# One-core encoder layer: the weight loads of the experts in another order in the queue

## The chip, the cores and the metric

The kernel runs on one core of one Trainium2 chip. The metric is the device time of one execution in microseconds (us); less is better. The core's engines are TensorE (PE in the profile, its weight loads PEld), VectorE (DVE), ScalarE (ACT), GpSimd (POOL) and SyncE (SP). SyncE computes nothing here: it waits on semaphores and issues DMAs, which 16 DMA engines carry out. "SPq" in a row is SyncE's sequencer.

## The reference

One encoder layer over 512 tokens of width 1024: three attention branches, a gated merge, and then the part that matters here, a layer of 32 experts of which each token uses four.

```python
def expert_block(args):
    xb, e = args
    gu = xb @ w_gu[e] + b_gu[e]                      # 1024 x 2048 per expert
    g = jnp.minimum(gu[:, :D_EXPERT], SWIGLU_LIMIT)
    lin = jnp.clip(gu[:, D_EXPERT:], -SWIGLU_LIMIT, SWIGLU_LIMIT)
    act = g * jax.nn.sigmoid(SWIGLU_ALPHA * g) * (lin + 1.0)
    return act @ w_down[e] + b_down[e]               # 1024 x 1024 per expert
```

Everything is float32. An expert's first matrix has 8 MB and its second 4 MB.

## The kernel before

The tokens of an expert are cut into jobs of up to 96 slots; there are 32 jobs here, numbered 0 to 31, and each job reads its expert's two matrices from HBM once. The first matrix comes in four pieces of 2 MB, the second in two. SBUF holds two full sets of four pieces for the first matrix (`gu_pair`, set 0 and set 1, taken in turn by even and odd jobs) and one set of two pieces for the second (`dn_pair`).

TensorE's order is fixed: `gate_up(0)`, and then in each step j `gate_up(j + 1)` (192 matmuls, L1783) followed by `down(j)` (192 matmuls, L1799), two steps to an iteration of its loop; after the loop come `gate_up(31)`, `down(30)` and `down(31)`. A part is one slice of weights: `gate_up` has eight parts and `down` four, and each part ends with an increment of `gemm_ps`. Two parts read one 2 MB piece, so a piece is free again when its second part is done. `gate_up` waits for each piece's `gu_in`, `down` for each piece's `dn_in`.

All weight loads are issued by SyncE, in one program order, onto one queue. SyncE waits until `gemm_ps` shows that a piece is free (`wait_part`) and then issues the next load into it. In the steady loop before the change, while step j runs, SyncE waits in `down(j)` for its two pieces, issues the two loads for `down(j + 1)` into them as they come free (after the second and the fourth part), and only then issues the four loads for `gate_up(j + 3)`, into pieces that `gate_up(j + 1)` had freed earlier in the same step:

```python
for m in range(GU_PAIRS):
    wait_part(sp, i, b * PARTS + 2 * m + 1)
    if m == 0:
        load_bias(e_gu, b)
    load_gu(e_gu, b, m)
for m in range(DN_PAIRS):
    wait_part(sp, i, stream(b, KD + 2 * m + 1))
    load_dn(e_dn, m)
```

GpSimd shares the same 16 DMA engines: in each step it adds the job's outputs to rows in HBM (`x_rows`, L964, small packets) and gathers the tokens of a coming job (`xq`, L958). These loads have a queue of their own ("software_dynamic", q0; SyncE's is q1, "hardware_dynamic").

Of the kernel before, what the change touches and what calls it, by code (L numbers as in the profile page):

```python
# [20 lines left out]
KD = D // P  # L21
# [11 lines left out]
N_EXP = 32  # L33
# [78 lines left out]
def encoder_kernel(nc, x, mem, norm_mix, w_in, q_norm_a, k_norm_a, sink_b, norm_mem, w_mem_kv,  # L112
# [3 lines left out]
    with ctx:  # L116
# [60 lines left out]
        def small(name, shape, dt):  # L177
            nonlocal at
            t = sb(name, shape, dt, at)
            size = int(np.prod(shape[1:])) * (2 if dt == BF16 else 4)  # L180
            at += -(-size // 32) * 32
            return t
# [105 lines left out]
        job_table = small("job_table", [1, 2, 64], I32)  # L288
# [258 lines left out]
        DN_PARTS = KD // 2  # L547
        GU_PAIRS = KD // 2
        DN_PAIRS = DN_PARTS // 2
        PARTS = KD + DN_PARTS  # L550
        G1 = GEMMS[UNITS]

        def stream(b, p):

            return KD + b * PARTS + p

        def wait_part(eng, i, m):
            eng.wait_ge(gemm_ps, i * (2 * PARTS) + (G1 + m + 1))
# [4 lines left out]
        def _(sp):  # L563
# [46 lines left out]
            def load_gu(e, s, m):  # L610
                sp.dma_start(gu_pair[s * GU_PAIRS + m][:], wgu[e, m, :, :]).then_inc(gu_in[s * GU_PAIRS + m], 16)

            def load_dn(e, m):
                sp.dma_start(dn_pair[m][:], wdn[e, m, :, :]).then_inc(dn_in[m], 16)

            def load_bias(e, s):
                for g in range(TRIOS):
                    sp.dma_start(bias_row[s][QUARTER * g:QUARTER * g + 8, :], bias_parts[e].rearrange("q r h n -> (q r) (h n)")).then_inc(bias_row_in[s], 16)
# [23 lines left out]
            e_one = sp.value_load(job_table[0:1, 0, 1:2], min_val=0, max_val=N_EXP - 1)  # L642
# [4 lines left out]
            sp.wait_ge(gate_t_ps, 1)  # L647
            load_gu(e_one, 1, GU_PAIRS - 1)
            pairs_but_one = sp.value_load(job_table[0:1, 1, 1:2], min_val=MIN_PAIRS - 1, max_val=NJ // 2 - 1)
            with sp.Fori(0, pairs_but_one) as i:  # L650
                for b in range(2):
                    e_gu = sp.value_load(job_table[0:1, 0, bass.ds(i * 2 + b + 2, 1)], min_val=0, max_val=N_EXP - 1)
                    e_dn = sp.value_load(job_table[0:1, 0, bass.ds(i * 2 + b + 1, 1)], min_val=0, max_val=N_EXP - 1)
                    for m in range(GU_PAIRS):
                        wait_part(sp, i, b * PARTS + 2 * m + 1)
                        if m == 0:
                            load_bias(e_gu, b)
                        load_gu(e_gu, b, m)
                    for m in range(DN_PAIRS):
                        wait_part(sp, i, stream(b, KD + 2 * m + 1))  # L660
                        load_dn(e_dn, m)
            e_last = sp.value_load(job_table[0:1, 0, bass.ds(pairs_but_one * 2 + 1, 1)], min_val=0, max_val=N_EXP - 1)
            wait_part(sp, pairs_but_one, stream(0, KD - 1))
            sp.dma_start(final_gain[:], norm_final.rearrange("(a n) -> a n", a=1).to_broadcast([P, D])).then_inc(fgain_in, 16)
# [18 lines left out]
        def _(act):  # L683
# [60 lines left out]
            def take_item(n):  # L744
                kind, _, slot = ITEMS[n]
                bank = 4 + n % 2 if n < 4 else 6 + (ITEM_STEP[n] // TB + 1) % 2
                act.wait_ge(qk_ps, n + 1)
                nc.scalar.activation(k_t[:] if kind == "k" else q_t[:, slot, :], ps[:, bank, :], ACT.Copy).then_inc(qk_done, 1)
# [1142 lines left out]
```

## Time and profile before

| | |
|---|---|
| median of 3 runs | 1474.77 us (1473.94 to 1475.23) |
| the profiled execution's own time | 1475.15 us |
| its span, first to last instruction | 1473.2 us |
| outside the span | 1.95 us |
| TensorE busy | 1448.4 us, 98% |
| VectorE, GpSimd, ScalarE busy | 464.4, 295.0, 270.4 us |
| moved by the DMA engines | 468.90 MB, of it 450.40 MB on SyncE's queue |

The expert stage runs from about 436 us to the end. Busy time of TensorE is modelled from the starts of its matmuls, so a high share alone doesn't say that it never waits; the idle time ahead of a group, and the chain that ended last, say more. "DMA share" in a row is the mean busy share of the 16 DMA engines; it can read a little over 1 where the packets of two queues overlap on an engine. One engine alone is a share of 0.0625.

### The profile page before, as it was taken

What the parts mean: (1) busy time and instruction counts of PE and PEld (TensorE: products, weight loads), DVE (VectorE), ACT (ScalarE), POOL (GpSimd) and SP (SyncE); (2) the same over time, 40 slices, a digit from 0 to 9 for tenths busy, and PEclk for the clock granted to TensorE, in tenths of its full rate; (3) what the DMA queues carried; (4) which work ended last, traced back from release to release, by engine and by line L of the source; (5) the groups of instructions that cost most, each with busy time, mean ns of one, the idle gap of its engine ahead of it and who ended that gap; (6) DMA issues with size and microseconds to landing.
All of it is one profiled execution on the core that took longest, in us unless ns stands there. A gap on an engine that the chain in (4) does not pass through costs nothing.

```text
span 1473.2 us, 34231 instructions
## 1 busy us (share of the span) xinstructions
PE 1448.4 (98%) x14951; PEld 754.4 (51%) x14951; DVE 464.4 (32%) x683; ACT 270.4 (18%) x491; POOL 295.0 (20%) x384
## 2 busy tenths in 40 slices
PE   8999999999999999999999999999999999999997
PEld 7876588888874344333344333344333344333344
DVE  4848833324561122211122211122211122211124
ACT  5458842233111010000010000010000010000011
POOL 0000040000012222233222233222233222232211
PEclk9999999999989999999999999999999999999999
DMA  7320013224959699999999999999999999999976
GB/s 257 138 86 1 23 49 123 90 72 138 377 211 419 255 413 418 413 415 412 415 420 414 417 416 412 416 415 416 418 413 412 415 417 414 419 414 412 414 292 243
DMA packets 71692, 468.90 MB, mean 318 GB/s; under 512 B 16040, under 2 KB 24772, under 8 KB 47040
## 3 DMA queue, kind: packets, MB, share of 16 engines
q1 hardware_dynamic: 52064, 450.40, 74.3%
q0 software_dynamic: 19104, 17.73, 5.5%
q8 instruction: 32, 0.52, 0.1%
q10 hardware_dynamic: 480, 0.15, 0.0%
q14 instruction: 12, 0.10, 0.0%
HBM read 458.33 MB, written 19.79 MB: 325 GB/s over the span
## 4 chain that ended last, share of the span: by engine, by line
PE 95%; DVE 3%; DMA 1%; ACT 0%; issue 0%; ACTq 0%; DVEq 0%; SPq 0%
PE ps L1783 45%; PE ps L1799 22%; PE ps L1433 7%; PE ps L1435 7%; PE ps L1434 7%; PE ps L1460 2%; PE ps L1586 1%; DVE head_max L1102 1%; PE ps L1774 1%; PE ps L1542 1%; DVE probs L1120 1%; DMA dn_pair<-in_w_down 1%; PE ps L1704 1%; PE ps L1469 0%; PE ps L1689 0%; DMA gain_rows<-in_norm_ffn 0%
## 5 line engine op out<-in xcount | busy, mean ns | idle before, releaser
L1783 PE MATMUL ps<-gu_pair,xt 128*32 128x512 f32 x6144 | 666.0, 593 | 0.5 <-ACT xt L859 0.5
L1783 PEld LDWEIGHTS ps<-gu_pair,xt 128*32 128x32 f32 x6144 | 197.1, 110 | 447.5 <-issue 446.7
L1799 PE MATMUL ps<-dn_pair,act_t 128*32 128x256 f32 x6144 | 339.1, 381 | 0.5 <-DMA dn_pair<-in_w_down 0.5
L1799 PEld LDWEIGHTS ps<-dn_pair,act_t 128*32 128x32 f32 x6144 | 201.0, 111 | 146.0 <-issue 20.2
L1336 DVE TENSOR_SCALAR lin_sb<-ps 128x768 f32<-128x768 f32 x32 | 30.6, 958 | 638.4 <-ACT sg_sb L865 638.4
L964 POOL DMA_INDIRECT x_rows<-y_sb,sum_row x93 | 147.9, 1591 | 37.8 <-issue 37.8
L941 POOL TENSOR_TENSOR mark_sb<-ones 1x1 f32<-1x1 f32 x93 | 30.3, 326 | 622.9 <-DVE y_sb L1352 617.8
L865 ACT ACTIVATE sg_sb<-ps,limits 128x768 f32<-128x768 f32 x32 | 28.8, 900 | 631.2 <-PE ps L1783 631.2
L1433 PE MATMUL ps<-w_high,h_hi 128*128 128x512 f32 x352 | 138.4, 393 | 0.6 <-DVE mem_lo L1048 0.5
L1435 PE MATMUL ps<-w_high,h_lo 128*128 128x512 f32 x352 | 137.3, 390 | 0.0
L1434 PE MATMUL ps<-w_low,h_hi 128*128 128x512 f32 x352 | 137.2, 390 | 0.0
L958 POOL DMA_INDIRECT xq<-h_rows,gather_row x93 | 96.6, 1039 | 38.2 <-issue 37.4
L518 DVE TENSOR_TENSOR w_low<-w_raw,w_high 128x2048 fp32r<-128x2048 f32 (+2 forms) x36 | 63.9, 1813 | 117.7 <-ACT w_high L510 117.7
L1433 PEld LDWEIGHTS ps<-w_high,h_hi 128*128 128x128 f32 x352 | 66.1, 188 | 14.8 <-DVE mem_lo L1048 0.8
L1435 PEld LDWEIGHTS ps<-w_high,h_lo 128*128 128x128 f32 x352 | 66.1, 188 | 13.9
L1434 PEld LDWEIGHTS ps<-w_low,h_hi 128*128 128x128 f32 x352 | 66.2, 188 | 13.2
L1352 DVE TENSOR_TENSOR y_sb<-ps,y_gate 128x768 f32<-128x768 f32 x31 | 29.7, 957 | 133.9 <-PE ps L1799 133.9
L870 ACT ACTIVATE y_gate<-slot_gates 128x3 f32 x32 | 6.6, 205 | 284.9 <-DVE y_sb L1352 280.4
L510 ACT ACTIVATE w_high<-w_raw 128x2048 fp32r<-128x2048 f32 (+2 forms) x36 | 53.5, 1538 | 20.3 <-PE ps L1435 17.6
L1344 DVE SCALAR_TENSOR_TENSOR act_sb<-lin_sb,sg_sb 128x768 f32<-128x768 f32 x32 | 48.9, 1528 | 3.3
L1332 DVE STREAM_TRANSPOSE xt<-xq 128x768 f32<-128x768 f32 x30 | 47.7, 1589 | 0.0
L972 POOL MEMSET limits<- 128x1 f32 x1 | 0.1, 98 | 215.8 <-DVE h L1181 215.8
(252 smaller groups left out, 962.5 us busy)
## 6 DMA issues: line engine op xcount, KB each, us to landing
gu_pair<-in_w_gate_up SPq DMA_DIRECT2D x128, 2048.0 KB, 22.2
dn_pair<-in_w_down SPq DMA_DIRECT2D x64, 2048.0 KB
w_raw<-in_w_in SPq DMA_DIRECT2D x8, 2048.0 KB, 8.0
w_raw<-in_w_out SPq DMA_DIRECT2D x2, 2048.0 KB, 7.7
w_raw<-in_w_in SPq DMA_DIRECT2D x2, 1024.0 KB, 8.1
x_sb<-in_x SPq DMA_DIRECT2D x8, 256.0 KB, 7.4
w_raw<-in_w_mem_kv SPq DMA_DIRECT2D x1, 2048.0 KB, 11.1
x<-in_x SPq DMA_DIRECT2D x4, 512.0 KB, 5.2
```

Source lines behind the costliest of these rows:

```text
L510: nc.scalar.activation(wh[u % 2][:, a * COLS:b * COLS], raw[u % 2][:, a * COLS:b * COLS], ACT.Copy).then_inc(wh_done, 1)
L518: nc.vector.tensor_tensor(wl[u % 2][:, a * COLS:b * COLS], raw[u % 2][:, a * COLS:b * COLS], wh[u % 2][:, a * COLS:b * COLS].bitcast(F32), ...
L958: nc.gpsimd.indirect_dma_start(out=xq[s][:, g, :], out_offset=None, in_=h2_rows.rearrange("r (q n) -> (r q) n", q=4), in_offset=bass.Indir ...
L964: nc.gpsimd.indirect_dma_start(out=x_rows.rearrange("r (q n) -> (r q) n", q=4), out_offset=bass.IndirectOffsetOnAxis(ap=sum_row[:, s, g:g ...
L1332: nc.vector.transpose(xt[:].rearrange("p g k t -> p (g k) t"), xq[s][:].rearrange("p g (i k) -> p g k i", k=KD)).then_inc(xt_done, 1)
L1336: nc.vector.tensor_scalar(lin_sb[:], ps[:, 0:TRIOS, QCOLS:2 * QCOLS], LIMIT, -LIMIT, ALU.min, ALU.max).then_inc(l_ready, 1)
L1344: nc.vector.scalar_tensor_tensor(out=act_sb[:].rearrange("p (c x) -> p x c", c=KD), in0=lin_sb[:].rearrange("p g (i c) -> p (g i) c", c=KD ...
L1433: nc.tensor.matmul(bank, hi, w_hi, start=start, stop=False)
L1434: nc.tensor.matmul(bank, hi, w_lo, start=False, stop=False)
L1435: return nc.tensor.matmul(bank, lo, w_hi, start=False, stop=stop)
L1783: last = nc.tensor.matmul(ps[quarter(q), g, :], xt[:, g, k, :], w.rearrange("p (h n) -> p h n", h=2)[:, :, q * QCOLS:(q + 1) * QCOLS], sta ...
L1799: last = nc.tensor.matmul(ps[quarter(q), bank + g, 0:QCOLS], act_part(2 * c + h, g), dn_w[c][:, h * D + q * QCOLS:h * D + (q + 1) * QCOLS] ...
```

## The change

Only SyncE's program changes. The four loads for `gate_up(j + 3)` are now issued one by one while `gate_up(j + 1)` reads the pieces, that is ahead of `down(j)` and ahead of the two loads for `down(j + 1)`. No load is added or removed, and no other engine's program changes.

```diff
-            with sp.Fori(0, pairs_but_one) as i:
+
+            def job_weights(i, b, e_gu, e_dn):
+                for m in range(GU_PAIRS):
+                    wait_part(sp, i, b * PARTS - DN_PARTS + 2 * m + 1)
+                    if m == 0:
+                        load_bias(e_gu, b)
+                    load_gu(e_gu, b, m)
+                for m in range(DN_PAIRS):
+                    wait_part(sp, i, b * PARTS + DN_PARTS + 2 * m + 1)
+                    load_dn(e_dn, m)
+
+            e_two = sp.value_load(job_table[0:1, 0, 2:3], min_val=0, max_val=N_EXP - 1)
+            for m in range(GU_PAIRS):
+                wait_part(sp, 0, 2 * m + 1)
+                if m == 0:
+                    load_bias(e_two, 0)
+                load_gu(e_two, 0, m)
+            e_three = sp.value_load(job_table[0:1, 0, 3:4], min_val=0, max_val=N_EXP - 1)
+            job_weights(0, 1, e_three, e_one)
+            with sp.Fori(1, pairs_but_one) as i:
                 for b in range(2):
                     e_gu = sp.value_load(job_table[0:1, 0, bass.ds(i * 2 + b + 2, 1)], min_val=0, max_val=N_EXP - 1)
-                    e_dn = sp.value_load(job_table[0:1, 0, bass.ds(i * 2 + b + 1, 1)], min_val=0, max_val=N_EXP - 1)
-                    for m in range(GU_PAIRS):
-                        wait_part(sp, i, b * PARTS + 2 * m + 1)
-                        if m == 0:
-                            load_bias(e_gu, b)
-                        load_gu(e_gu, b, m)
-                    for m in range(DN_PAIRS):
-                        wait_part(sp, i, stream(b, KD + 2 * m + 1))
-                        load_dn(e_dn, m)
+                    e_dn = sp.value_load(job_table[0:1, 0, bass.ds(i * 2 + b, 1)], min_val=0, max_val=N_EXP - 1)
+                    job_weights(i, b, e_gu, e_dn)
+            e_next = sp.value_load(job_table[0:1, 0, bass.ds(pairs_but_one * 2, 1)], min_val=0, max_val=N_EXP - 1)
+            for m in range(DN_PAIRS):
+                wait_part(sp, pairs_but_one, DN_PARTS + 2 * m + 1)
+                load_dn(e_next, m)
```

Inside the loop both programs issue four loads of a first matrix and then two of a second. What differs is which second matrix follows which first one, and that is decided where the loop is entered. On SyncE, the first time that a second matrix is loaded in the stage, the program before has these rows (`dn_pair` 166 and 167 are the two pieces of the second matrix, `gu_pair` 158 to 161 set 0 and 162 to 165 set 1 of the first):

```order
L614 DMA dn_pair_167<-in_w_down 128x4096
L652 ISA
L652 TENSOR_LOAD job_table
L652 ISA x2
L653 TENSOR_LOAD job_table
L653 ISA x2
L558 REGISTER_ALU
L618 ISA [waits gemm_ps]
L618 DMA bias_row_113<-bias_parts 8x512 x3
L611 ISA
L611 DMA gu_pair_162<-in_w_gate_up 128x4096
```

The second matrix of job 1 stands ahead of the first matrix of job 3, which goes into set 1. At the same place the changed program has:

```order
L618 DMA bias_row_113<-bias_parts 8x512 x3
L611 ISA
L611 DMA gu_pair_162<-in_w_gate_up 128x4096
L611 ISA [waits gemm_ps]
L611 DMA gu_pair_163<-in_w_gate_up 128x4096
L611 ISA [waits gemm_ps]
L611 DMA gu_pair_164<-in_w_gate_up 128x4096
L611 ISA [waits gemm_ps]
L611 DMA gu_pair_165<-in_w_gate_up 128x4096
L614 ISA [waits gemm_ps]
L614 DMA dn_pair_166<-in_w_down 128x4096
```

Job 3's first matrix has moved ahead of job 1's second, and each of its loads has a wait of its own. The loop keeps this order to its end. Behind the loop, on SyncE, the program before goes straight to the loads of the tail:

```order
L662 ISA
L662 TENSOR_LOAD job_table
L662 ISA x2
L558 ISA
L664 DMA final_gain<-in_norm_final 128x1024 [waits gemm_ps]
L666 DMA down_bias<-in_b_down 32x1024 x4
L558 REGISTER_ALU
L614 ISA [waits gemm_ps]
L614 DMA dn_pair_166<-in_w_down 128x4096
```

and the changed program first issues the second matrix of job 30, which no first matrix precedes any more:

```order
L674 ISA
L674 TENSOR_LOAD job_table
L674 ISA x2
L558 ISA
L614 ISA [waits gemm_ps]
L614 DMA dn_pair_166<-in_w_down 128x4096
L558 REGISTER_ALU
L614 ISA [waits gemm_ps]
L614 DMA dn_pair_167<-in_w_down 128x4096
```

So each second matrix but the last two has one first matrix more ahead of it in the queue than before.

## Rows read from the trace of the kernel before

**Rows 1.** The page: busy time, and the two groups of expert matmuls (last field: idle time before)

```profile
PE 1448.4 (98%) x14951; PEld 754.4 (51%) x14951; DVE 464.4 (32%) x683; ACT 270.4 (18%) x491; POOL 295.0 (20%) x384
...
L1783 PE MATMUL ps<-gu_pair,xt 128*32 128x512 f32 x6144 | 666.0, 593 | 0.5 <-ACT xt L859 0.5
...
L1799 PE MATMUL ps<-dn_pair,act_t 128*32 128x256 f32 x6144 | 339.1, 381 | 0.5 <-DMA dn_pair<-in_w_down 0.5
```

**Rows 2.** The chain that ended last, late jobs: start, length, what

```profile
1368.92 10.36 PE ps L1799 x192
...
1379.71 20.74 PE ps L1783 x192
1400.45 10.36 PE ps L1799 x192
...
1437.37 8.03 DMA dn_pair<-in_w_down
...
1445.44 12.30 PE ps L1799 x192
```

**Rows 3.** SyncE's timeline, first jobs: start, length, what is issued

```profile
453.17 9.09 SPq L611 DMA_DIRECT2D gu_pair<-in_w_gate_up  x4
491.41 5.51 SPq L614 DMA_DIRECT2D dn_pair<-in_w_down  x2
...
499.84 1.99 SPq L611 DMA_DIRECT2D gu_pair<-in_w_gate_up  x4
522.94 5.51 SPq L614 DMA_DIRECT2D dn_pair<-in_w_down  x2
```

**Rows 4.** SyncE's timeline, last jobs

```profile
1374.30 5.51 SPq L614 DMA_DIRECT2D dn_pair<-in_w_down  x2
...
1382.72 2.00 SPq L611 DMA_DIRECT2D gu_pair<-in_w_gate_up  x4
1405.83 5.51 SPq L614 DMA_DIRECT2D dn_pair<-in_w_down  x2
...
1437.37 5.54 SPq L614 DMA_DIRECT2D dn_pair<-in_w_down  x2
```

**Rows 5.** The third load of three first matrices: when issued, and time to landing

```profile
L611 SPq DMA_DIRECT2D gu_pair<-in_w_gate_up x1: 333/333/333, 501.0 to 501.0; - x1
...
DMA to landing us min/median/max: 21.4/21.4/21.4
...
L611 SPq DMA_DIRECT2D gu_pair<-in_w_gate_up x1: 333/333/333, 1194.7 to 1194.7; - x1
...
DMA to landing us min/median/max: 30.3/30.3/30.3
...
L611 SPq DMA_DIRECT2D gu_pair<-in_w_gate_up x1: 333/333/333, 1383.9 to 1383.9; - x1
...
DMA to landing us min/median/max: 32.7/32.7/32.7
```

**Rows 6.** Stretches in early jobs: engines' busy time, clock, DMA share, GB/s

```profile
478.00:479.00 1.00, 1.00 (x15) 0.28 (x10) 0.00 (x0) 0.00 (x0) 0.00 (x0) 1.00 0.84 305
...
481.50:492.00 10.50, 10.50 (x160) 5.07 (x156) 4.78 (x4) 1.84 (x2) 0.00 (x0) 1.00 0.01 2
```

**Rows 7.** The same view, end of the job loads

```profile
1431.00:1432.00 1.00, 1.00 (x16) 0.34 (x12) 0.00 (x0) 0.00 (x0) 0.00 (x0) 1.00 0.08 34
1432.00:1433.00 1.00, 1.00 (x24) 0.64 (x20) 0.00 (x0) 0.87 (x1) 0.00 (x0) 1.00 0.01 1
```

**Rows 8.** DMA over one job, 1347.67 to 1379.20 us, and a GpSimd add later

```profile
DMA packets 1468, 13.04 MB, mean 414 GB/s; under 512 B 298, under 2 KB 598, under 8 KB 718
...
q0 software_dynamic: 576, 0.70, 9.4%
...
1412.92 1.63 POOL L964 DMA_INDIRECT x_rows<-y_sb,sum_row  x1 [0.55 <-issue]
```

**Rows 9.** The stretch behind TensorE's wait near the end

```profile
1446.00:1458.00 12.00, 11.69 (x188) 6.42 (x180) 0.00 (x0) 0.24 (x1) 3.77 (x3) 0.86 0.82 265
```

## The prediction

> **What bounds the kernel now.** I read the page first. TensorE is busy for 1448.4 of 1473.2 us, and the idle time ahead of both groups of expert matmuls is 0.5 us in all [rows 1]. Busy time is modelled, so this alone proves little. The chain of work that ended last settles it: `down` starts at 1368.92 and again at 1400.45 us, 31.53 us apart, and the chain stays on TensorE between them [rows 2]. So a job costs 31.53 us of matmuls in the loop, and no wait for a weight is in it. Only at the end does the chain go over a load: 8.03 us for the second matrix of job 31, of which about 5.2 us lie beside the second half of `down(30)`.
>
> Second question: how close are the loads to being late? Over one job the DMA engines move 13.04 MB at 414 GB/s [rows 8], which is 31.5 us. The loads are thus almost as long as the matmuls. The landing times tell more. A load has landed when the slowest of its 16 shares has. The third load of a first matrix landed 21.4 us after its issue at 501.0 us, 30.3 us after it at 1194.7, and 32.7 us after it at 1383.9 [rows 5]. Issue stands in the same place of a job each time, so the backlog grows by (32.7 - 21.4) / 28 jobs = 0.40 us per job: the slowest share needs 31.53 + 0.40 = 31.93 us of work for each job. The end of the stage shows how few engines this concerns: between 1431 and 1432 us the DMA share is 0.08, little more than one engine of 16, and that one is done at about 1432.2 (share 0.01 in the next us) [rows 7]. I call it the last engine. Before the change its backlog is harmless: it is never late by the time at which TensorE reads.
>
> The Trainium skill, "DMA: Bandwidth & Descriptors", section "Latency and other measured facts", says that DMA engines 7 and 15 are usually slower than the others. The rows don't name the engine, but that one or two lag agrees with it.
>
> **The change, part by part.** TensorE, ScalarE, VectorE and GpSimd keep their programs: 0 us. SyncE issues as many loads as before; it has some 20 us of waiting between its groups of issues [rows 4], which hides its extra waits and table reads: 0 us. Memory is the same.
>
> What it adds to a second matrix is queue. Each share of a load waits behind the earlier loads on its engine. Before, the second matrix of job 30 (issued at 1405.83) was the last behind the first matrix of job 31 (1382.72), and the one of job 29 (1374.30) stood ahead of it [rows 4]. Now job 31's first matrix stands ahead of job 29's second.
>
> *What has to be done by when.* The second piece of job 29 is read from the third part of `down(29)` on: 1400.45 + 10.36 / 2 = 1405.6 us [rows 2]. After the change, everything up to the first matrix of job 31 and the second of job 29 has to be through by then. Before, the last engine was through this same set of loads when the fourth load of job 31's first matrix had landed. The third landed at 1383.9 + 32.7 = 1416.6 [rows 5]; three loads later, at 1432.2, it was done with everything [rows 7], so 15.6 / 3 = 5.2 us per load, and the fourth landed at 1421.8.
>
> *What it gains at the start.* The queue was empty once. Job 2's first matrix was issued from 453.17 us, and then nothing until 491.41 [rows 3]. The share falls from 0.84 in 478 to 479 us and is 0.01 over 481.5 to 492 [rows 6]: the first engines ran dry at about 478.3, the last at about 481.3, and with 1.1 us from issue to the first packets (taken as the start at 492.5, where that stretch ends) they stood still for 11 to 14 us. The changed program issues job 3's first matrix from about 470 us, while `gate_up(1)` reads, so this gap fills, and from then on the last engine is ahead of its former self by 11 to 14 us. The engine that lags at the end most likely lagged at the start too, so I take 11.5.
>
> *What else shifts.* The q0 traffic takes 9.4% of the engines' time, 3.0 us per job [rows 8]. It is tied to TensorE's time, not to the queue. The adds issued from 1412.92 us on [rows 8] slowed the load that landed at 1421.8; in the new order it is past before they come. I take a quarter of a job's 3.0 us, 0.7 (0 to 1.5).
>
> *The sum.* 1421.8 - 11.5 - 0.7 = 1409.6 us, against a need at 1405.6: **4.0 us late**. By the same working at the load issued at 1194.7: 1194.7 + 30.3 + 5.2 - 12.2 = 1218.0, need 189.1 us before 1405.6, i.e. 1216.5: 1.5 us late. So the first wait should come some four jobs earlier, near 1090 us, and from then on each job waits 0.4 us for its second matrix. The ends: advance 14 and shift 1.5 give 0.7 us, advance 11 and shift 0 give 5.2.
>
> *Given back?* Job 30's second matrix has no first matrix ahead of it any more, and job 31's is issued and lands as before, 8.03 us later [rows 2, 4]. Nothing behind job 29 is late, and nothing makes up the 4.0 us: the matmuls of the rest lie on the chain. First matrices come earlier, but no `gate_up` waited for one (0.5 us idle in all, and that on ScalarE [rows 1]), so earlier arrival gains 0.
>
> Against the profiled execution (1473.2 us span, 1475.15 with what lies around it) this makes 1477.2 and 1479.15. That execution is 0.4 us over the median, so I forecast 1474.8 + 4.0 = **1478.8 us**.
>
> *The rule that speaks against the change.* The last engine's landing times grow steadily though TensorE takes weights at a constant pace [rows 5]: a load waits for all that was issued ahead of it. The Trainium skill, "DMA: Bandwidth & Descriptors", section "Queues, rings and completion order", says that on each DMA engine descriptors are consumed in ring order. Without the gap at the start this rule would make the sum 11.5 us larger, 15.5 us late; the empty stretch in this case's trace [rows 6] cuts it to 4.0.
>
> **The rivals.**
>
> *No wait at all: same time.* For it: only about one engine is late by this much (share 0.08 near the end [rows 7]), and if its extra work comes from four loads issued within 2 us [rows 4] beside the adds, evenly spread loads may take less than 31.93 us per job. It decides if it needs 31.93 - 4.0 / 28 = 31.79 us or less per job: a third less drift, 0.26 instead of 0.40. Also, runs without the profiler may drift less than this one. Against it: the growth is steady, (30.3 - 21.4) / 22 = 0.40 us per job up to 1194.7 and (32.7 - 30.3) / 6 = 0.40 from there on [rows 5]. Time: 1474.8 us.
>
> The Trainium skill, "DMA: Bandwidth & Descriptors", section "Where 436 GB/s comes from", gives a ceiling of 435.2 GB/s. An estimate from it is 13.04 MB / 435.2 GB/s = 30.0 us per job, under the matmuls' 31.53; by that rule the queue would never grow and the change would cost 0. The measured 414 GB/s and the growing landing times [rows 5, 8] say otherwise for the slowest share, and the measurement decides.
>
> *Larger loss.* If TensorE's waits bring its clock down: behind the wait near the end, the granted clock is 0.86 over 12 us [rows 9], a loss of 12 x 0.14 = 1.7 us, with part of it at 1.2 instead of 2.4 GHz. That wait comes out of 8.03 us in which TensorE had only 5.2 us of work. Waits of 0.4 us are far smaller and I don't expect it; if three or four did it, 4.0 + 3.5 x 1.7 gives about +10 us, 1484.8.
>
> *Faster.* The change would have to take away a wait that is in the chain. There is one for weights, the 8.03 us ahead of `down(31)`, and its issue hangs on `down(30)` in both programs. If the last engine's earlier finish cut a bit of the landing time, at most 8.03 - 5.2 = 2.8 us could go; that needs a queue that still holds it up at 1437, and it was empty since 1432.2 but for the small loads of the tail. Time then 1472.0.
>
> *The change does nothing.* Excluded: the order of issue shows the first matrix ahead of the second.
>
> **How the numbers follow.** A measurement of this kernel tells about 0.2% from no change, 2.95 us. The waits as worked out (0.7 to 5.5 us): 0.66, of which 0.13 is under 2.95 us. No wait: 0.24. Larger loss: 0.07. Faster: 0.03. So slower 0.53 + 0.07 = 0.60, same 0.13 + 0.24 = 0.37, faster 0.03. The range goes from the no-wait case, 1474.3 with the spread of the runs, to 1480.8, a little over the upper end of the sum; the larger loss stays out. The forecast's own range is 1475.5 to 1480.3.
>
> **What the changed profile would show.** The engines busy at 481.5 to 492 us (share near 1). Job 1's second matrix landing some 16 us after its issue (481.3 + 5 loads x 5.3 = 507.8, issued at 491.4), and job 29's 26 us after it, when it is needed (1400.45 - 1374.30). In the chain, from about 1090 us on, pieces "DMA dn_pair" between `gate_up` and `down`, or a `down` longer than 10.36 us, 0.4 us per job and 4 us in all; `gate_up` unchanged; clock at 1.00 in the loop. The last load for job 29 is the last late one. I am wrong if `down` stays at 10.36 us everywhere (the last engine's drift is smaller in the new order), if waits are there from the first jobs (no gap was filled), or if it is `gate_up` that waits.

## The result, and the profile after

The changed kernel takes 1480.59 us (median of 6 runs, 1479.15 to 1482.51) against 1475.21 (1473.94 to 1475.68, 6 runs): ratio 1.0038, 95% interval 1.0026 to 1.0050. It is slower by 5.4 us. The profiled execution took 1482.51 us, with a span of 1480.7.

The page of the changed kernel has TensorE still at 98%. What has moved is the idle time ahead of the matmuls of `down` (last field, L1815 here, L1799 before), where [rows 1] had 0.5 us, and that of their weight loads:

```profile
L1799 PE MATMUL ps<-gu_pair,xt 128*32 128x512 f32 x6144 | 667.4, 594 | 0.5 <-ACT xt L875 0.5
...
L1815 PE MATMUL ps<-dn_pair,act_t 128*32 128x256 f32 x6144 | 341.0, 381 | 3.7 <-DMA dn_pair<-in_w_down 3.5
L1815 PEld LDWEIGHTS ps<-dn_pair,act_t 128*32 128x32 f32 x6144 | 199.1, 110 | 153.6 <-DMA dn_pair<-in_w_down 15.0
```

`gate_up` waits for nothing, as before. Ahead of a wait, the sequencer still has matmuls in the array, so the 3.5 us of matmul idle time and the 15.0 us of weight-load idle time (20 waits) frame the loss. The chain gives it more closely. It stays on TensorE until 1117 us, job after job as in [rows 2], and then:

```profile
1117.31 5.18 PE ps L1815 x96
...
1122.51 5.43 PE ps L1815 x96
...
1128.10 26.58 DMA dn_pair<-in_w_down
...
1154.72 5.43 PE ps L1815 x96
...
1160.30 26.36 DMA dn_pair<-in_w_down
...
1379.37 26.75 DMA dn_pair<-in_w_down
...
1406.16 10.57 PE ps L1815 x192
...
1417.17 20.74 PE ps L1799 x192
...
1443.29 8.41 DMA dn_pair<-in_w_down
```

The chain hardly runs through `gate_up` any more: from 1128 to 1379 us it goes from the issue of a second piece to its landing 26.4 to 26.8 us later, then through half a `down`, which frees the piece for the next issue (only at 1353 us does it pass through one `gate_up`, and behind it, for `down(29)`, it is the first piece that is late). Two such steps start 1160.30 - 1128.10 = 32.2 us apart, the later ones 32.0 to 32.1, where matmuls alone need 31.53. `down(29)` starts at 1406.16, against 1400.45 in [rows 2]; 0.66 us of that was there before the loop (465.96 against 465.30 us for the start of `gate_up(1)`): in this execution TensorE idled 2.34 us for the gather of the first tokens, its granted clock was at the lower level (0.51) from 434.9 to 438.4 us, and the first 72 matmuls of `gate_up(0)` took 9.36 us instead of 7.93. `down(29)` ends at 1416.73, where before it ended at 1410.81: with the 0.66 off, 5.3 us are lost in the loop. The other 1.6 us by which the two spans differ lie behind it (0.4 of it in the last second matrix, 8.41 instead of 8.03 us, and 1.2 behind `down(31)`). The medians, 5.4 us apart, are close to the loop's loss alone.

The view of stretches shows that stretch of lower clock (first line) and the gap of [rows 6] filled:

```profile
434.90:438.40 3.50, 3.01 (x16) 0.79 (x20) 3.12 (x5) 0.44 (x1) 2.25 (x2) 0.51 0.49 112
...
478.00:479.00 1.00, 1.00 (x16) 0.32 (x12) 0.00 (x0) 0.00 (x0) 0.30 (x1) 1.00 1.03 363
...
481.50:492.00 10.50, 10.50 (x156) 4.77 (x148) 4.12 (x4) 1.84 (x2) 0.00 (x0) 1.00 1.01 422
```

and the third load of a first matrix, the view of [rows 5], is issued some 15 to 20 us earlier and needs as long as all that stands in the queue. The three are the loads of jobs 3, 25 and 31:

```profile
L611 SPq DMA_DIRECT2D gu_pair<-in_w_gate_up x1: 333/333/333, 481.7 to 481.7; - x1
DMA to landing us min/median/max: 15.5/15.5/15.5
...
L611 SPq DMA_DIRECT2D gu_pair<-in_w_gate_up x1: 333/333/333, 1176.3 to 1176.3; - x1
DMA to landing us min/median/max: 25.8/25.8/25.8
...
L611 SPq DMA_DIRECT2D gu_pair<-in_w_gate_up x1: 333/333/333, 1368.9 to 1368.9; - x1
DMA to landing us min/median/max: 26.3/26.3/26.3
```

### The profile page after: what moved, and what is told of

The parts are those of the page before. It is cut to its first block, busy times and chain, and to the rows that moved or that the text cites. A ratio compares the mean times of both kernels' runs of the same rounds, so it can differ in the third digit from the quotient of the medians.

```text
span 1480.7 us, 34258 instructions
## 1 busy us (share of the span) xinstructions
PE 1447.7 (98%) x14951; PEld 746.5 (50%) x14951; DVE 464.1 (31%) x683; ACT 270.5 (18%) x491; POOL 295.0 (20%) x384
## 3 DMA queue, kind: packets, MB, share of 16 engines
q0 software_dynamic: 19104, 17.73, 5.5%
## 4 chain that ended last, share of the span: by engine, by line
PE 80%; DMA 16%; DVE 3%; issue 0%; ACT 0%; ACTq 0%; DVEq 0%; SPq 0%; POOLq 0%
PE ps L1799 34%; PE ps L1815 20%; DMA dn_pair<-in_w_down 15%; PE ps L1449 7%; PE ps L1451 7%; PE ps L1450 7%; PE ps L1476 2%; PE ps L1602 1%; DVE head_max L1118 1%; PE ps L1558 1%; PE ps L1790 1%; DVE probs L1136 1%; DMA xg<-h_rows,gather_row 0%; PE ps L1485 0%; PE ps L1705 0%
## 5 line engine op out<-in xcount | busy, mean ns | idle before, releaser
L1799 PE MATMUL ps<-gu_pair,xt 128*32 128x512 f32 x6144 | 667.4, 594 | 0.5 <-ACT xt L875 0.5
L1799 PEld LDWEIGHTS ps<-gu_pair,xt 128*32 128x32 f32 x6144 | 196.7, 110 | 449.4 <-issue 448.5
L1815 PE MATMUL ps<-dn_pair,act_t 128*32 128x256 f32 x6144 | 341.0, 381 | 3.7 <-DMA dn_pair<-in_w_down 3.5
L1815 PEld LDWEIGHTS ps<-dn_pair,act_t 128*32 128x32 f32 x6144 | 199.1, 110 | 153.6 <-DMA dn_pair<-in_w_down 15.0
```

Source lines behind the costliest of these rows:

```text
L1799: last = nc.tensor.matmul(ps[quarter(q), g, :], xt[:, g, k, :], w.rearrange("p (h n) -> p h n", h=2)[:, :, q * QCOLS:(q + 1) * QCOLS], sta ...
L1815: last = nc.tensor.matmul(ps[quarter(q), bank + g, 0:QCOLS], act_part(2 * c + h, g), dn_w[c][:, h * D + q * QCOLS:h * D + (q + 1) * QCOLS] ...
```

## The experiments

Eight kernels tell the order in the queue, the gap at the start, the spacing and the traffic apart; three more (e3, e9, e10) vary the dose. Times are medians beside runs of the kernel before on the same chip.

### e1: second matrices on a queue of their own

```diff
-                for m in range(DN_PAIRS):
-                    wait_part(sp, i, b * PARTS + DN_PARTS + 2 * m + 1)
-                    load_dn(e_dn, m)
...
                     sigmoid(j + 1)
+                    e_dn = act.value_load(job_table[0:1, 0, bass.ds(i * 2 + b + 1, 1)], min_val=0, max_val=N_EXP - 1)
+                    for m in range(DN_PAIRS):
+                        wait_part(act, i, stream(b, KD + 2 * m + 1))
+                        act.dma_start(dn_pair[m][:], wdn[e_dn, m, :, :]).then_inc(dn_in[m], 16)
```

> The changed kernel, with the second matrices of jobs 1 to 30 issued by ScalarE on its own queue instead of by SyncE; same bytes, same 16 engines, first matrices as early as in the changed kernel. My theory (a second matrix is late because one first matrix more stands ahead of it in the same queue): on a queue of its own it shares each engine with the first matrices instead of waiting behind them, so about 2 us + 2 x 4.9 us = 12 us from issue to landing against the 26 us at which it is needed; no wait ahead of down, 31.53 us per job to the end, 1475.2 us. Rival (the last DMA engine can't carry the loads of a job in a job's time, whatever their order): down still waits from about 1120 us on, 1480 us. If ScalarE's issuing costs time of its own, it shows in down or in the sigmoid, not as a wait for dn_pair.

Measured: 1474.57 us against 1474.62, ratio 0.9995 (0.9986 to 1.0005). Its chain at the place where the changed kernel loses time, and ScalarE's issue in the timeline:

```profile
1368.96 10.36 PE ps L1812 x192
1379.32 0.43 PE ps L1787 x3
1379.76 20.74 PE ps L1796 x192
1400.49 10.36 PE ps L1812 x192
...
712.18 5.51 ACTq L902 DMA_DIRECT2D dn_pair<-in_w_down  x2
```

The first matrices are issued as early as in the changed kernel and the same 16 engines carry the same bytes, but a job takes 31.53 us again. The loss thus came from what stands ahead in the one queue. By the landing records, a first piece took 14.1 to 14.8 us from issue to its slowest share and a second one 18.3 to 19.8 (jobs 1 to 29), more than the 12 that I expected and well under 26. The last engine still falls behind in e1: the third load of a first matrix lands 17.3 us after its issue for job 3 and 37.1 us after it for job 31. The lateness has moved to loads that can bear it; it hasn't gone.

### e2: the gap at the start kept

```diff
             e_three = sp.value_load(job_table[0:1, 0, 3:4], min_val=0, max_val=N_EXP - 1)
+            wait_part(sp, 0, DN_PARTS + PARTS + 1)
             job_weights(0, 1, e_three, e_one)
```

> The changed kernel, with the first matrix of job 3 held back until down(0) has read its first piece (about 491 us), so that the DMA engines stand still as long as in the kernel before; the order in the queue is that of the changed kernel. My theory (backlog: the early issue gave the last engine 11.5 us of advance against 21 us more ahead of each second matrix): without the advance TensorE is 11.5 us later than in the changed kernel, 1480.6 + 11.5 = 1492 us, with waits ahead of down from the first jobs on (second matrix of job 1 landing some 27 us after issue). Rival (only the growth per job counts, not where it starts): 1480.6 us, first wait near 1120 us.

Measured: 1498.76 us against 1474.62, ratio 1.0160 (1.0143 to 1.0177), 18 us over the changed kernel. The stretch is empty again, and the chain waits at the first chance:

```profile
481.50:492.00 10.50, 10.50 (x168) 5.15 (x164) 4.87 (x4) 1.84 (x2) 0.00 (x0) 1.00 0.01 3
...
495.20 26.70 DMA dn_pair<-in_w_down
...
521.95 13.07 PE ps L1816 x192
```

`down(1)` takes 13.07 us instead of 10.36, and that is the clock: TensorE idled 4.95 us before it, from 517.0 to 521.95 us, its granted clock was at the lower level (0.50) from 520.2 to 527.0 us, and `down(1)` got through only 48 of its 192 matmuls in the 5.05 us of that stretch in which it ran.

```profile
521.95 13.07 PE L1816 MATMUL ps<-dn_pair,act_t 128*32 128x256 f32 x192 [4.95 <-DMA dn_pair<-in_w_down]
...
520.20:527.00 6.80, 5.05 (x48) 2.37 (x52) 2.76 (x2) 0.00 (x0) 0.00 (x0) 0.50 1.01 398
```

The second piece had landed by 527.5 us, before `down(1)` came to it. Where the backlog starts decides, as my theory had it; the rival is out. The size was off: not 11.5 but 18 us. By the landing records 14.6 of them stand at job 1's second matrix (through at 527.5 us, against 513.0 in the changed kernel), and the rest has come by job 29's (1428.9 against 1411.0).

### e3, e9, e10: some pieces ahead, the others behind

```diff
-                for m in range(GU_PAIRS):
+                for m in range(GU_PAIRS // 2):
                     wait_part(sp, i, b * PARTS - DN_PARTS + 2 * m + 1)
...
                     load_dn(e_dn, m)
+                for m in range(GU_PAIRS // 2, GU_PAIRS):
+                    load_gu(e_gu, b, m)
```

with 1 and 3 in the place of `GU_PAIRS // 2` in e9 and e10.

> The changed kernel, with the third and fourth piece of each first matrix issued behind the second matrix, the first two ahead of it. My theory: 2 x 5.2 = 10.4 us less stand ahead of a second matrix, and the gap at the start fills nearly as well, so the end of job 29's load comes some 9 us earlier than in the changed kernel, 4 us ahead of its need; no wait at all, 1475.2 us. Rival (each piece moved ahead costs its share): half the loss, 1478 us.

Measured: 1478.95 us against 1474.62, ratio 1.0030 (1.0021 to 1.0040). Both expectations failed: half the dose costs 4.3 us, four fifths of the whole loss. The backlog began as low as I had worked out (the first one landed 8.6 us after issue at 492 us), but it grew nearly twice as fast, and the waits came all the same:

```profile
1211.38 10.59 PE ps L1817 x192
...
1222.12 26.91 DMA dn_pair<-in_w_down
```

> The changed kernel with one piece of each first matrix issued ahead of the second matrix and three behind it. The last engine's backlog grew by 0.46 us per job with no piece ahead, 0.8 with two (e3) and 0.55 with four. Theory A (the growth comes with cutting the first matrix in two parts around the second): 0.7 to 0.8 us here, from 9 us at first to 26 us some 22 jobs later, then waits, 1478 to 1479 us. Theory B (it grows with what stands ahead): 0.5 us, 23 us at the end, no wait, 1475 us.

Measured: 1482.06 us against 1475.39, ratio 1.0044 (1.0027 to 1.0061), growth 1.0 us per job: more than either theory.

> The same with three pieces ahead and one behind. 15.6 us more ahead, of which 11.5 filled the gap at the start: the second matrix of job 1 lands some 13 us after issue. Theory A (cut in two): 0.7 to 0.8 us of growth per job, the need of 26 us reached after 17 jobs and 11 jobs of waits, 1482 to 1484 us, more than the changed kernel's. Theory B: growth 0.5 us, reached after 26 jobs, 1476 us.

Measured: 1476.69 us against 1475.39, ratio 1.0007 (0.9998 to 1.0017), growth 0.65 us. Theory A had the time much too long; theory B had the time (1476 us) and the place at which waits begin (1311 us, 26 jobs on), but not the growth. The loss is not a matter of how many pieces are moved: 0, 1, 2, 3, 4 pieces ahead cost 0, 6.7, 4.3, 1.3 and 5.4 us, of which the times alone don't tell 1.3 from nothing; that e10 waits is seen in its trace, where `down` is idle 1.9 us for `dn_pair`.

### e4, e11: the spacing of the issues

e4 is the kernel before with its first matrices issued 5.2 us apart, e11 the changed kernel with them issued two and two:

```diff
-                        wait_part(sp, i, b * PARTS + 2 * m + 1)
+                        wait_part(sp, i, b * PARTS + KD + 2 * m + 1)
...
-                    wait_part(sp, i, b * PARTS - DN_PARTS + 2 * m + 1)
+                    wait_part(sp, i, b * PARTS - DN_PARTS + 4 * (m // 2) + 3)
```

> The kernel before, in its order, but each piece of a first matrix is issued a part of gate_up later, 5.2 us apart, instead of four at once behind down. It asks why the last engine's backlog grew by 0.55 us per job after the change and 0.40 before. If the spacing of the issues is the cause: 0.55 us per job here too. If it is the order or what stands in the queue: 0.40 us per job. Either way second matrices land 9 us after issue at first and at most 24 at the end, under the 26 they have, so no wait and 1475.2 us.

Measured: 1474.87 us against 1474.62, ratio 1.0003 (0.9993 to 1.0013). The first pieces of its second matrices landed 11.0 us after issue at 489 us and 22.6 at 1403, which is 0.40 us per job.

> The changed kernel in its order, but the four loads of a first matrix are issued two and two (after the fourth and the eighth part of gate_up) instead of one by one. If only the order in the queue and the bytes count: as the changed kernel, growth 0.55 us per job, 1480 to 1481 us. If the evenly spaced issue is what raised the growth from 0.46 to 0.55: growth 0.46 to 0.50, some 2 us less, 1478 to 1479 us.

Measured: 1481.11 us against 1475.39, ratio 1.0041 (1.0027 to 1.0055). With the order before, spacing the issues brings neither waits nor faster growth; with the new order, bunching them takes neither away (waits begin at 999 us, even earlier than at 1122). Even spacing is out as a cause, of the loss and of the faster growth.

### e5 to e8: GpSimd's traffic left out

One bound is changed, in `add_rows` for e5 and e7 and in `gather_quarters` for e6 and e8; e5 and e6 start from the changed kernel, e7 and e8 from e3:

```diff
-                                                 in_=y_sb[:, g, :], in_offset=None, bounds_check=4 * SEQ - 1, oob_is_err=False,
+                                                 in_=y_sb[:, g, :], in_offset=None, bounds_check=0, oob_is_err=False,
```

> The changed kernel, with the bounds of GpSimd's adds into x_rows set so that they write next to nothing (the experts' outputs of jobs 0 to 30 are left out of the result; every wait and every matmul stays). In the changed kernel the last engine needs about 32.1 us of work per job against 31.53 us of matmuls. My theory: that overload is the traffic of GpSimd's queue on top of 6 x 4.9 us = 29.4 us of weights; the adds take 30 us of packet time per job, 1.9 us per engine. Without them about 30.2 us per job, so the backlog shrinks from job to job instead of growing, no wait ahead of down, 1475 us. Rival (the weight loads alone are too slow on that engine): waits from about 1120 us on as before, 1480 us.

> The changed kernel, with the bounds of GpSimd's gathers of the tokens of jobs 2 to 31 set so that they read next to nothing (those jobs compute with old data; waits and matmuls stay). The gathers take 15 us of packet time per job, 1.0 us per engine. My theory: 32.1 - 1.0 = 31.1 us per job on the last engine, under 31.53, no waits, 1475 us. It also asks what makes some of the 16 KB weight packets slow (mean 620 ns against 611 at best, most of the excess in the stretch in which the gathers run): if it is the gathers, the excess in that stretch goes and the engine has still more room; if it stays, something else makes it.

Measured: 1474.91 us (ratio 1.0005, 0.9995 to 1.0014) without the adds and 1475.07 (1.0004, 0.9994 to 1.0013) without the gathers, against 1474.64. Their pages, e5 first, show what was taken off the queue (17.73 MB and 5.5% of the engines' time in the changed kernel) and that `down` has next to no wait left:

```profile
q0 software_dynamic: 19104, 9.80, 2.4%
...
L1815 PE MATMUL ps<-dn_pair,act_t 128*32 128x256 f32 x6144 | 339.1, 380 | 0.8 <-DMA dn_pair<-in_w_down 0.8
```

```profile
q0 software_dynamic: 19104, 9.85, 4.3%
...
L1815 PE MATMUL ps<-dn_pair,act_t 128*32 128x256 f32 x6144 | 339.1, 380 | 1.0 <-DMA dn_pair<-in_w_down 1.0
```

By the landing records, a second matrix took 14 to 16 us in the first jobs and 9.0 and 9.5 at 1348 us: the backlog shrinks. In the changed order the weights with one kind of GpSimd's traffic are not too much for the last engine, with both kinds they are; the rival, that the weights alone are too much, is out.

> The kernel with two pieces ahead (e3), adds left out as in e5. In e3 the last engine's backlog grew by 0.8 us per job instead of 0.46, with a mean weight packet of 624 ns instead of 619. Theory A: slower weight packets come from meeting the gathers; they stay at some 624 ns here, and the backlog no longer grows because 1.9 us of adds per job are gone. Theory B: they come from meeting the adds; the mean falls to some 615 ns. Either way no wait, 1475 us.

> The kernel with two pieces ahead (e3), gathers left out as in e6. Theory A (the slow weight packets meet the gathers): the mean weight packet falls from 624 to some 615 ns and the backlog doesn't grow, 1475 us. Theory B (they meet the adds): the mean stays at 624 ns, the last engine's work per job falls by 1.0 us of gathers alone, from 32.4 to 31.4 us, just under the 31.53 that it has, 1475 us with landing times that stay as they are.

Measured, one run each: 1472.35 and 1473.23 us, no waits in the loop. In e7 the backlog doesn't grow (second matrices land 7.1 to 9.2 us after issue, with no trend). In e8 it still does, from 7.4 to 16.0 us between 584 and 1346 us, 0.3 us per job, where 31.4 us of work per job had been expected and would have let it shrink; it stays short of 26. On the slow weight packets both theories failed: the mean is 638 ns without adds and 628 without gathers, higher than with both.

### The growth, side by side

From the landing records of the second piece of each second matrix (issued from 640 to 1060 us, a line fitted over the jobs) and from all 16 KB weight packets of that time: growth of the slowest share's landing time in us per job, mean packet, and share of packets over 640 ns. There is one trace for each kernel, and in some, that of the kernel before among them, a few landing records are missing, so small differences of growth say little.

```
                        growth   packet   over 640 ns
before (0 ahead)         0.50     617.9     3.7%
e4 (0 ahead, spaced)     0.44     617.7     3.4%
changed (4 ahead)        0.57     620.2     6.8%
e11 (4 ahead, in twos)   0.69     620.8     6.6%
e10 (3 ahead)            0.65     620.8     7.4%
e3 (2 ahead)             0.95     623.8     9.9%
e9 (1 ahead)             1.01     624.9    10.0%
```

In these kernels a larger growth goes with slower weight packets: 48 packets of a job and engine times 7 ns are 0.34 us of the 0.51 us between e9 and the kernel before. That is an agreement of two columns, not a cause: e5, e7 and e8 have slower packets yet (628 to 638 ns) and a growth of 0.3 us at most, and e1 has fast ones (617.5 ns) though the landing times of its first matrices grow.

## Why the prediction was right or wrong

**Mechanism: right.** The step "one first matrix more ahead of it in the queue" is what costs: e1 takes the queue away and the loss with it. The waits are ahead of `down` alone, second matrices land at the 26 us that they have, the clock stays at 1.00 in the loop, job 29's is the last late one, and nothing is given back. SyncE's extra waits cost nothing, as forecast. Job 1's second matrix took 15.3 us to land, forecast some 16. The first late load stands at 1122 us, forecast near 1090, and each job from there on loses 0.5 to 0.6 us, forecast 0.4: fewer waits, and longer ones.

**The gap at the start: right in kind, too small.** I let the filled gap advance the last engine by 11.5 us and shifted 0.7 more of GpSimd's traffic, 12.2 in all. The rows give the real one. Job 3's third load landed at 501.0 + 21.4 = 522.4 us before [rows 5] and at 481.7 + 15.5 = 497.2 after; of these 25.2 us, two loads of 5.2 are the second matrix that no longer stands ahead of it, and 14.8 are advance. So the term was 2.6 us too small, in favour of the change. That the gap counts is shown by e2, whose second matrix of job 1 lands 14.6 us later than in the changed kernel.

**The growth: the step that was mis-sized.** "The slowest share needs 31.93 us of work for each job", and the sum took this to hold in the new order as well, by reading the end of the queue off the trace of before. It doesn't: at job 31's third load the same reckoning gives 1383.9 + 32.7 = 1416.6 before, 1368.9 + 26.3 = 1395.2 after, 21.4 us less 10.4 is 11.0. The advance of 14.8 us had shrunk by 3.8 us over 28 jobs: 0.14 us of work per job more on the last engine, 32.07 instead of 31.93 us. Put into the prediction's own sum, 1421.8 - 11.0 - 1405.6 = 5.2 us late, where the forecast had 4.0. The two errors, 2.6 us one way and 3.8 the other, cancelled in part, and that the forecast came this near is owed to that.

That 5.2 nearly meets the chain's 5.3 is in part luck, too. TensorE ran 0.66 us later in this execution, which moves the need to 1406.3 us and leaves 4.6; and the last wait was not for the second piece of job 29, as the sum had it, but for the first, which landed at 1406.12 us where it could have been read at 1401.1. Nor is the 0.14 us a steady rate. By the third load the advance is 14.8 us at job 3, 14.0 at job 21, just before the first wait, and 11.0 at job 31; by the last load that has to be through it is 14.7, 12.4 and 10.9. How much of the extra work comes from the order and how much from the waits themselves, the traces don't tell; between 640 and 1060 us, where nothing waits, the growth is 0.57 against 0.50 us.

**The rival "no wait at all"** needed 31.79 us per job or less in the new order. It went the other way, and its argument, that loads issued in bursts make the extra work, fell with e4, where loads 5.2 us apart left the growth at 0.40 us per job. What it had right is the cause of the overload: without the adds, or without the gathers, there is no wait (e5, e6). The estimate of 30.0 us per job from the Trainium skill's ceiling ("DMA: Bandwidth & Descriptors", "Where 436 GB/s comes from") is refuted for this mix by the growing landing times and by the waits. **The larger loss** by a falling clock did not come: waits of about half a microsecond per job leave it at 1.00 (mean granted clock from 1128 to 1406 us). In e2, where TensorE idled 4.95 us at a stretch, the clock did fall, to 0.50 for 6.8 us. **Faster** had nothing to take away, and e1 shows that early first matrices gain nothing even when they delay nobody.

**What stays open.** Why the last engine's work per job depends on the order at all, and why one piece ahead is the worst order (1.0 us per job) and three the cheapest of the moved ones. The runs exclude the even spacing of the issues, and tie the overload to the traffic of GpSimd's queue, but not the difference between the orders: leaving out either kind of traffic did not bring the weight packets back to 618 ns. Open too is which engine is the last one, and whether it is the same all along: the landing records don't name it.

## What to carry to other kernels

Where one queue feeds two buffers, issue in the order in which the data is needed: a load that is needed 57 us after its issue and stands ahead of one that is needed after 26 turns the spare time of the first into lateness of the second. A TensorE at 98% with no waits can sit next to a DMA engine that falls behind by half a microsecond per job, and the view to find that in is the time from issue to landing of the same load in an early and in a late job. Don't carry that growth over to another order of the same bytes as if it were a constant: measured between 0.5 and 1.0 us here, it was the largest error of the forecast.

## What the runs showed of the hardware

The 16 shares of a load drift apart. In the kernel before, the second piece issued at 1411 us had landed with its first share after 7.8 us and with its last after 21.8, at equal bytes per engine, and what set TensorE's pace after the change was that last one, while the mean throughput hardly differed (416 GB/s before and 414 after, from 640 to 1060 us). A second queue is served beside a long first one: in e1 a 2 MB load landed within 14 to 20 us though about as many loads of the other queue were in flight as in the changed kernel, where it took up to 26.8. The price is paid by the other queue, whose loads took up to 37 us.
